# Products of the identity ahead of x and of its last pair of tiles in a fused encoder block

## What is computed

```
x = x + 0.5 * swiglu(rms_norm(x, ffn1_norm), ffn1_w_gate, ffn1_w_up, ffn1_w_down)
h = rms_norm(x, mix_norm)
proj = h @ w_in            # z, xBC, dt, u
x = x + concat(ssd_group(...), multiscale_pool_group(...)) @ w_out
x = x + 0.5 * swiglu(rms_norm(x, ffn2_norm), ffn2_w_gate, ffn2_w_up, ffn2_w_down)
return rms_norm(x, final_norm)
# swiglu(h) = (silu(h @ w_gate) * (h @ w_up)) @ w_down
```

## Time and profile before

| what | value |
|---|---|
| median of 3 runs | 1046.6 us (1046.41 to 1046.92) |
| profiled execution, its own time | 1046.38 us |
| its span, first to last instruction | 1044.6 us |
| what lies around the span | 1.78 us |
| PE busy | 1028.0 us |
| DVE busy | 567.2 us |
| ACT busy | 380.5 us |
| POOL busy | 191.2 us |
| mean DMA rate | 95 GB/s |

### The profile page before, as it was taken

The page is one execution under the profiler, slowest core; times in us unless marked ns, Lnnn a source line. Parts: engine busy times, 40 slices in busy tenths (PEclk is TensorE's granted clock), DMA queues, the critical chain, the costliest instruction groups (busy, mean ns, idle before and its releaser), DMA issues.

```text
span 1044.6 us, 13522 instructions
## 1 busy us (share of the span) xinstructions
PE 1028.0 (98%) x4776; PEld 843.2 (81%) x4776; DVE 567.2 (54%) x677; ACT 380.5 (36%) x485; POOL 191.2 (18%) x174
## 2 busy tenths in 40 slices
PE   6999999999999999999999999999999999999997
PEld 4888888888888878878787888888888888888887
DVE  7554444444444368787699795554444444434432
ACT  6333322233333336663234653333322233232332
POOL 5011011011010031321063451110100101101100
PEclk9999999999999999999999999999999999999999
DMA  6443333322332433323322233333333233233322
GB/s 186 118 123 98 100 100 93 89 89 68 99 96 83 127 102 101 101 61 82 81 81 63 79 90 112 96 89 97 100 100 98 84 99 90 71 111 92 93 68 81
DMA packets 188809, 99.08 MB, mean 95 GB/s; under 512 B 3716, under 2 KB 188136, under 8 KB 188776
## 3 DMA queue, kind: packets, MB, share of 16 engines
q1 hardware_dynamic: 186520, 96.03, 31.8%
q10 hardware_dynamic: 2256, 2.62, 0.8%
HBM read 96.54 MB, written 2.10 MB: 94 GB/s over the span
## 4 chain that ended last, share of the span: by engine, by line
PE 94%; DVE 4%; issue 1%; ACT 1%; DMA 0%; ACTq 0%
PE bank L1070 29%; PE bank L1072 29%; PE bank L1071 29%; DVE xglo L697 1%; PE bank L1125 1%; DVE w_lo_part L692 1%; PE bank L1387 0%; PE bank L1200 0%; PE bank L1222 0%; PE bank L1389 0%; PE bank L1388 0%; PE bank L1190 0%; DVE ebuf L823 0%; DVE xT L725 0%; DMA xload<-in_x 0%
## 5 line engine op out<-in xcount | busy, mean ns | idle before, releaser
L1070 PE MATMUL bank<-xghi,w_hi_part 128*128 128x512 f32 x976 | 384.0, 393 | 0.0
L1072 PE MATMUL bank<-xghi,w_lo_part 128*128 128x512 f32 x976 | 380.1, 389 | 0.0
L1071 PE MATMUL bank<-xglo,w_hi_part 128*128 128x512 f32 x976 | 379.9, 389 | 0.0
L692 DVE TENSOR_TENSOR w_lo_part<-w_raw,w_hi_part 128x1024 fp32r<-128x1024 f32 x198 | 260.6, 1317 | 192.9 <-ACT w_hi_part L467 187.6
L467 ACT ACTIVATE w_hi_part<-w_raw 128x1024 fp32r<-128x1024 f32 x198 | 207.9, 1051 | 199.9 <-PE bank L1072 195.3
L1070 PEld LDWEIGHTS bank<-xghi,w_hi_part 128*128 128x128 f32 x976 | 183.2, 188 | 40.9 <-issue 3.1
L1071 PEld LDWEIGHTS bank<-xglo,w_hi_part 128*128 128x128 f32 x976 | 183.3, 188 | 38.8 <-issue 1.4
L1072 PEld LDWEIGHTS bank<-xghi,w_lo_part 128*128 128x128 f32 x976 | 183.2, 188 | 38.5
L378 POOL TENSOR_TENSOR gate_buf<-gate_buf,rstd 128x512 f32<-128x512 f32 x44 | 57.1, 1298 | 407.1 <-ACT gate_buf L492 407.1
L1070 PE MATMUL bank<-acthi,w_hi_part 128*128 128x512 f32 x330 | 130.5, 396 | 0.0
L1072 PE MATMUL bank<-acthi,w_lo_part 128*128 128x512 f32 x330 | 129.4, 392 | 0.0
(11 more groups left out here) (209 smaller groups left out, 763.8 us busy)
## 6 DMA issues: line engine op xcount, KB each, us to landing
w_raw<-in_ffn_w_gate SPq DMA_DIRECT2D x44, 512.0 KB, 3.8
w_raw<-in_ffn_w_up SPq DMA_DIRECT2D x44, 512.0 KB, 3.8
w_raw<-in_w_in SPq DMA_DIRECT2D x29, 512.0 KB, 3.8
w_raw<-in_ffn_w_down SPq DMA_DIRECT2D x32, 384.0 KB, 3.2
w_raw<-in_ffn_w_down SPq DMA_DIRECT2D x32, 320.0 KB, 3.0
w_raw<-in_w_out SPq DMA_DIRECT2D x16, 512.0 KB, 3.6
xload<-in_x ACTq DMA_DIRECT2D x4, 512.0 KB, 5.6
out<-xtok SPq DMA_DIRECT2D x4, 512.0 KB, 3.1
```

Source lines behind the costliest of these rows:

```text
L692: dve.tensor_tensor(wlo[:, slot(m)], raw[:, slot(m)], whi[:, slot(m)].bitcast(F32), ALU.subtract).then_inc(w_lo, 1)
L1070: pe.matmul(bank, w, h, start=first and n == 0, stop=False)
L1071: pe.matmul(bank, w, l, start=False, stop=False)
L1072: mm = pe.matmul(bank, wl, h, start=False, stop=last and n == blocks - 1)
```

## The change

A helper `keep_warm(n)` on PE issues n products of the identity with itself, 128 columns each, float32, into the first 128 columns of bank 6; nothing reads them, and nothing is signalled. It is called with 6 after the wait for the constants and ahead of the transpose of the gain row, with 12 ahead of x's first tile, and with 6 ahead of x's tile 6, whose transposes then write the same bank. Nothing is taken away, no wait is added and no other engine's list is changed.

```diff
--- before.py
+++ after.py
@@ -1107,7 +1107,12 @@
+            def keep_warm(n):
+                for _ in range(n):
+                    pe.matmul(PB[6][:, 0:P], ident[:, :], ident[:, :], start=True, stop=True)
+
             pe.wait_ge(consts, 4)
+            keep_warm(6)
             pe.wait_ge(norm_landed, 16)
             pe.transpose(PB[7][:, 0:DK], prow[0:DK, :], ident[0:DK, 0:DK]).then_inc(par_T, 1)
@@ -1134,7 +1139,10 @@
+            keep_warm(12)
             for d in range(DK):
+                if d == 6:
+                    keep_warm(6)
                 x_tile(d)
             pe.wait_ge(w_hi, 1)
```

## The result

The changed kernel takes 1050.43 us in the median of 8 executions (1049.48 to 1050.87), against 1046.99 (1046.41 to 1048.49) of the kernel before in as many. The ratio is 1.0032, 95% interval 1.0022 to 1.0041: slower by 3.4 us. The profiled execution took 1050.39, with a span of 1048.7. It is typical of its kernel, 0.04 under the median, while the profiled execution of the kernel before, at 1046.38, lies 0.61 under this median of 1046.99. So a comparison of the two profiles gives a delay of 4.0 us where the medians give 3.4.

A forecast was written before the change was run, and what follows sets the result against it. The prediction took PE as the bound, its full stretch set by tile 0 through DVE's list. Tile 0 2.9 us later made span 1047.5, plus 1.78 gives 1049.3, plus 0.22 to the median 1049.5; range 1048.5 to 1050.9.

The forecast's parts named there:

- The sign: Whole kernel: slower by more than the 2.1 us a measurement can tell, chance 0.85; x can't start on landing at 4.48.
- the price of a product: On PE: two records per float32 product, 0.433 us at the lower clock level and 0.223 at the higher.
- The forecast's condition: At PE's start: clock rises between 4.5 and 7 us, delay 2.3 to 3.4 us, chance 0.62.
- rival A: At PE's start: clock rises late, at 7 to 9 us; 3.5 to 4.6 us later, 1050.1 to 1051.2; chance 0.21.
- The bound: PE full from 22.07 us, paced before by DVE's list, entered through tile 0 alone; tile 0's 2.9 us delay stays.
- The start at 2.0: PE's first product starts at 2.0 us, after the fourth constant; 2.4 if the gain row's load is awaited.
- The moment of the clock: At PE's start: pace doubles at 5.8 us, 3.8 after PE's first work at 2.0.
- Rival B: Products ahead of x are cheap, mean below 0.276 us each; tile 0 under 2.1 us late, no measurable slowdown; chance 0.12.
- 0.51 us for a warm first tile: Tile 0's four transposes at the fast clock take 0.62 us instead of 1.13, giving 0.51 back.
- The last six: Products ahead of tile 6: 1.34 us on PE, hidden by cover of over 4 us before DVE asks at 17.8.
- The gain row: Its transpose ends at 4.75 us, 2.3 later than before; gains ready by 6.5, wanted past 9, costing nothing.
- It stays there through the idle 1.8 us.: PE's clock stays at the higher level through the idle 1.8 us ahead of 12.88.

The follow-up runs named there:

- e10_fill_third: The kernel of e8_fill measured a third time, seven products in PE's waits of unit 0 against the kernel before: 1046.99 us.
- e4_moved: Against the changed kernel, the first six products gone and the 12 moved from ahead of x to ahead of tile 4: 1046.96 us.
- e11: The changed kernel itself, unaltered, profiled once more to read the moment of the clock: 1050.81 us.
- e1: Against the changed kernel, only the six products ahead of the gain row's transpose are left: 1047.21 us.
- e5: Against the changed kernel, 24 products ahead of x instead of 12: 1052.69 us.
- e7: Against the changed kernel, 48 products ahead of tile 6 instead of 6: 1052.78 us.
- e12: The changed kernel itself, unaltered, profiled another time after e11: 1050.34 us.
- e6_bf16: Against the changed kernel, the same 24 products in the same places, on the identity's words read as bfloat16: 1046.73 us.
- e8_fill: Against the kernel before, seven products of the identity in PE's waits for DVE inside unit 0, none ahead of x: 1046.60 us.
- e2_twelve: Against the changed kernel, only the 12 products ahead of x are left: 1049.39 us.
- e9_fill_again: The kernel of e8_fill measured a second time, for the count of long executions: 1046.60 us.
- e3_last6: Against the changed kernel, only the six products ahead of tile 6 are left: 1047.17 us.

## Why the prediction was right, point by point

Forecast 1049.5 in a range from 1048.5 to 1050.9; measured 1050.43, slower as forecast, by 3.4 instead of 2.9.

The sign, the path and the price of a product were right by their reasons. That the number came so near has luck in it. The forecast's condition was a clock that rises between 4.5 and 7; it rose between 7 and 9, as rival A has it, in four of the six profiles named below, and 1050.43 lies among rival A's 1050.1 to 1051.2. The range holds it because its upper end was put over most of A. And the delay of 3.4 looks nearer to 2.9 than the profiles' 4.0 does, since the kernel before had a median of 1046.99 here, not the 1046.6 that the forecast adds to. A late first load of x is one cause of its longer executions (0.35 us at the first copy of e10_fill_third), which 18 products hide; that it explains the whole 0.4 isn't shown.

- **The bound.** Right. The path enters through tile 0 alone, and from the first copy to the last instruction the old chain ran unchanged. e4_moved is the direct test: the same products behind tile 3 cost nothing.
- **The price of a product.** Two records each, right. 0.217 and 0.112 a record were taken from transposes and from line 1287; 0.213 and 0.112 were measured. The first six with the gain row behind them ended at 5.05 instead of 4.75, and the next burst again lost 0.17 at its head: the first records are further apart than the price in a stream. That start, 0.47 late in all, is 0.25 us at tile 0, since a later start leaves fewer slow records.
- **The start at 2.0.** Right (1.99).
- **The moment of the clock.** This is the term that was mis-sized. It was put at 5.8, from one execution and the assumption that it follows PE's first work by 3.8 us. It was 7.9 in the profiled execution, and 5.4, 6.3, 7.1, 7.5 and 7.7 in five others whose float32 products began at 1.99 (e11, e1, e5, e7, e12): 3.4 to 5.9 us after the first. The 3.8 was also counted from x's first transpose, at 4.53. PE's first record was the gain row's transpose at 2.42, which the rise followed by 5.8 to 6.0 us; from 2.0 that would have given 7.8 to 8.0. The spread shows that neither count is a rule. At 0.47 us each, 7.9 for 5.8 is 1.0 us, and with the 0.25 it makes up the 1.22 between the worked-out end of tile 0, 8.57, and the measured 9.79. The profiled execution (1050.39) and e12_changed_look (1050.34) are rival A's case, and the median stands beside them. e11_changed_look is the forecast's case at the first copy, 8.63 for 8.6, but not in its time, for the fall at 26.
- **Rival B**, a cheap product, is what e6_bf16 makes of it: true for bfloat16, not for float32. Its side remark, 0.51 us for a warm first tile, didn't come true there, because the clock was not up.
- **The last six** were covered, as worked out: done by 14.2, asked for at 18.82. The cover of over 4 us was confirmed by e7_cover48's wait, but the wait's way to the end was not one to one.
- **The gain row.** ACT's copy came at 5.16, behind a table load that did not wait (2.97, as in the earlier trace rows), so the gains were ready at 5.3 rather than 6.5, and nobody missed them.
- **"It stays there through the idle 1.8 us."** True of that trace, and wrong as a rule. In e8_fill the same idle stretch ahead of 12.87 was followed by a granted clock of 0.57 from 14 to 16 us, at no cost there, because DVE is the bound; and so was e2_twelve's, behind an idle 2.93, by one of 0.50 from 16 to 18. The fall between 23 and 30 goes with 1.6 us in all three profiles that have it. The prediction saw no place where products could help; here may be one, if the hint of e8_fill to e10_fill_third holds, and it would be needed in one execution of ten.

The rule of the Trainium skill that was weighed ("TensorE: Matmul & The Clock Gate", Part 4, that transposes don't bring the full clock) is contradicted again by e9_fill_again, where x's 32 transposes took 5.88 us from 4.57, less than the 6.9 of the slow price, with nothing but transposes before them.

## What to carry to other kernels

A filler ahead of the first input is free only until the input lands. Add up its records at the slow price, two per float32 product, before placing it, and place it where the engine's result isn't awaited: the same twelve products cost 2.5 us at one place and nothing four tiles later. Ask what the faster clock would buy: here at most 0.51 us at the first tile, while a fall of the clock just ahead of the dense part, which costs 1.6, was not thought of. And before a forecast rests on a moment read from one execution, read it from several: here it differed by 2.5 us, worth 1.2 us of the time.

## What the runs showed of the hardware

- The moment at which PE's pace doubles differs from execution to execution of the same kernel: 5.4, 7.7 and 7.9 us in three of the changed one, with the same work up to 5 us.
- The granted clock's column reads 1.00 from the start, also where records are 0.213 us apart; only a later fall shows in it as 0.50. At the start of a program the pace must be read from the records.
- In e3_last6 the clock fell between 23.0 and 23.5 us although PE had had no wait longer than 0.96 us since 4.82; it had been busy for 3.5 of the six us up to 22. The kernel before was busy for 3.24 of the same six and kept 1.00. The Trainium skill, in "TensorE: Matmul & The Clock Gate" under "Why this matters for your kernels", asks that long idle gaps between bursts of products be kept out against drops in mid-kernel; this run shows a fall without one.
- One remainder of x (line 697) takes 0.68 us on DVE in e7_cover48, where POOL is idle, and 1.49 for the same tiles in the kernel before, where POOL adds.
- The first small load came in at 2.4 us in some executions and at 3.4 in others, x's first pair with it at 4.5 or 4.8. The kernel before follows it by 0.3 us; behind the changed kernel's 18 products x is taken up at 9.2, 8.0 and 9.1, long after either.
